# Input projections in pairs by Strassen's scheme ahead of a state-space scan

## The chip, the cores and the metric

The kernel runs on one core of one Trainium2 chip. The metric is device time in microseconds (us) of one execution; the kernel before took 2148.05 us as the median of three runs (2147.49 to 2153.19).

## What is computed

One inference step of a hybrid decoder layer, for a prompt of 1024 tokens and 8 single-token samples, 1032 rows in all, in float32:

```python
u = rmsnorm(x, norm_w)
proj = u @ w_in                      # 1024 -> 14368 columns
cb, cc, ch, cz, sz, sxbc, sdt, mq, mz, gr = jnp.split(proj, idx, axis=-1)
conv_out, new_buf_a = causal_conv(cc * ch, buf_a, conv_a_w)
y_a = (jax.nn.silu(cz) * cb * conv_out) @ w_a_out
xbc, new_buf_s = causal_conv(sxbc, buf_s, conv_s_w, conv_s_b)
...
y, h_new = ssd_scan(xs, dt, a, bm, cm, h0)
y_s = gated_rmsnorm(y + d_skip * xs, sz, ssm_norm_w) @ w_s_out
o = mem_attention(mq, mk, mv)
y_m = (jax.nn.silu(mz) * o) @ w_m_out
merged = g[:, :, 0] * y_a + g[:, :, 1] * y_s + g[:, :, 2] * y_m
return x + merged @ w_o, ...
```

In tiles of 128 columns the projection has 113 of them: 24 of xBC, 1 of dt, 16 of the scan's gate z, 8 each of cc, ch, cz and cb, 8 of q, 8 of the attention's gate and 24 of merge gates. The scan is chunked: 8 chunks of 128 tokens, 4 groups of 8 heads in each, every group adding to a state that the next chunk's group reads.

## The kernel before, in words

The program is written out engine by engine, with semaphores between them. TensorE (PE) multiplies, VectorE (DVE) does elementwise work, ScalarE (ACT) reads results out of PSUM and issues stores, GpSimd (POOL) splits weights, SyncE (SP) issues loads, all strictly in the order written.

**A projection tile** (`dense`, L195): float32 accuracy comes from a split of each operand in a high and a low part, and three products (high-high, low-high, high-low) for each of 8 blocks of the inner dimension. The 1032 rows are three pieces of 344, so a tile is 72 matmuls of 344 columns into three PSUM banks (`acc`). Its weights are loaded by SP (`load_w`, L171), split by POOL with one `tensor_scalar` and one `tensor_tensor` of 128x1024 (`split_w`, L176, L181, L183), and the pieces are read out by ACT (`read_out`, L207) or DVE.

**Order of the stages.** First the rows of x are normed, transposed and split (`turn_rows`, `high_rows`, `low_rows`); the first tile's pieces are multiplied in between. Then come the 24 xBC tiles, each followed on DVE by a four-tap convolution (L975 to L990: a `tensor_scalar` and three `scalar_tensor_tensor` of 128x1024, the same on 8 columns for the samples, and a copy of the tail), and by SiLU and a store on ACT. Then dt, two z tiles, 8 more z tiles mixed with 16 tiles of memory keys and values (product with 256 columns, tile `mhi`), transposes of keys and values, and 6 late z tiles (`late_z`). While these late tiles run, SP stores what the scan reads back (`s_cs`, `s_kt`, `s_bc`, outputs) and loads the first group.

**The scan** (PE from L1441, ACT from L795, DVE from L1112, SP from L520). For each group PE waits for `group_in` (the group's loads) and for `h_added` (the state of the group before; it frees bank `pm0`), transposes x (L1450) and b (L1452), forms the scores (L1453), runs one dense tile, transposes z (L1457), waits for DVE's masked decay matrix `mm_` (`m_ready`), does the three scan products (L1462 to L1465, `summed`), then one or two more dense tiles (`SEG`: 2, 2, 2 and 3 tiles in the groups of a chunk, 9 in all), and transposes the group's normed output (L1470). DVE for a group: decay arguments, eight `seg` rows, copies of b and scores, scaled x, `mm_` (L1119 to L1137); after `summed` the output and the state (L1143 to L1153, the state's addition is L1148), the norm's factor (L1157 to L1164), and a step of the samples' own state (`sample_step`, L1065 to L1068, in groups 0 and 2; `sample_output`, L1073 and L1075, after it). DVE also does the short convolution's arithmetic on four of the nine tiles (`dve_tile`).

SP's order in a group: x and z of the group, the decay rows broadcast to all partitions (`s_cs`), the weights of the group's tiles, and in groups 0 and 2 the sample state (`in_state_ssm`), in group 0 also the broadcast b and c of the samples (`s_bc`, 1 MB). The `s_bc` load waits until the chunk before has finished with `sd_step`, and all later loads stand behind it on SP.

**After the scan** four passes of output projections with attention beside them, and the last product with `w_o`.

Of the kernel before, what the change touches and what calls it, by code (L numbers as in the profile page):

```python
# [45 lines left out]
ZT, XT = INNER // P, XBC // P  # L46

# [17 lines left out]
def build(nc, I, O):  # L65
# [18 lines left out]
    with ExitStack() as ctx:  # L84
# [8 lines left out]
        pm = [ctx.enter_context(nc.psum_tensor(f"pm{i}", [P, 512], F32)) for i in range(5)]  # L93
        uhi = sb("uhi", [P, KT, T], F32R)
        ulo = sb("ulo", [P, KT, T], F32R)

# [12 lines left out]
        ident = sb("ident", [P, P])  # L109
        tri = sb("tri", [P, P])  # L110
        ones = sb("ones", [P, P])
        epsc = sb("epsc", [P, 1])
        par = sb("par", [P, NPAR])
        hist_s = sb("hist_s", [P, XT, NB, KS - 1])
        hist_a = sb("hist_a", [P, KT, NB, KA - 1])
        tail_s = sb("tail_s", [P, XT, TAIL_S])
        tail_a = sb("tail_a", [P, KT, TAIL_A])
        cs_tok = sb("cs_tok", [P, NCH * HEADS])
        dt_tok = sb("dt_tok", [P, NCH * HEADS])
        dskip = sb("dskip", [P, HEADS])  # L120
# [106 lines left out]
        xbc_tile = lambda i, r: (i, r, i * 3 + r)  # L227
        Q1 = XT // 3
        dt_tile, z_first = (Q1, 0, XT), [(Q1, 1, XT + 1), (Q1, 2, XT + 2)]

        mixed_tile = lambda i, j: (i * 2 + Q1 + 1 + j // 3, j % 3, None if j % 3 else i * 2 + XT + 3 + j // 3)
        late_z = lambda i, r: (i + Q1 + 9, r, i * 3 + XT + 11 + r)
        QM, FM = Q1 + 11, XT + 1 + ZT
        main_tile = lambda c, m: (c * 3 + QM + m // 3, m % 3, c * 9 + FM + m)

        xbc_src = lambda j: w_in[:, :, bass.ds(j * P + O_XBC, P)]
        z_src = lambda j: w_in[:, :, bass.ds(j * P + O_SZ, P)]
        kv_src = lambda j: w_kv[:, :, bass.ds(j * P, P)]
        MAIN = (O_CC, O_CH, O_CZ, O_CB, O_MQ, O_MZ, O_G, O_G + D, O_G + 2 * D)
        rows = lambda d, j: d[bass.ds(j * P, P), :]  # L240


        rows_in = [sem(f"rows_in{b}") for b in range(2)]
        par_in, hist_in, small_in = sem("par_in"), sem("hist_in"), sem("small_in")
        square_done, root_done, rs_done = sem("square_done"), sem("root_done"), sem("rs_done")
        normed = [sem(f"normed{b}") for b in range(2)]
        turned, u_high, u_split = sem("turned"), sem("u_high"), sem("u_split")
        par_turned, par_copied, norm_in = sem("par_turned"), sem("par_copied"), sem("norm_in")
        PROMPT_ROWS = SEQ // P + 1
        xr = [view(D), view(D)]  # L250
        xn = [view(D), view(D)]
        nwb, mwb = view(D), view(D)
        junk = view(D)
        par_rows = view(2, P)
        hrow_s, hrow_a = view(XBC), view(D)
        ssq, root, rs = view(16), view(16), view(16)
        NROW = SEQ // P + 1 + NM // P
        def row_tile(a):

            if a < SEQ // P:  # L260
                return P, I["x_prompt"][0, a * P:(a + 1) * P, :], a * P
            if a == SEQ // P:
                return NB, I["x_sample"][:, 0, :], SEQ
            a -= SEQ // P + 1
            return P, I["mem_prompt"][0, a * P:(a + 1) * P, :], a * P
        def turned_rows(a, h):

            n, _, c0 = row_tile(a)
            hi, lo = (uhi, ulo) if a < PROMPT_ROWS else (mhi, mlo)
            src = pm[2 * (a % 2) + h][:, :].rearrange("p (k c) -> p k c", c=P)[:, :, 0:n]  # L270
            return src, hi[:, 4 * h:4 * h + 4, c0:c0 + n], lo[:, 4 * h:4 * h + 4, c0:c0 + n]

        xp = view(T + KS - 1, at=M0 + 15900)
        cv = view(T)
        dtb, alog = view(1), view(1)
        conv = [sem(f"conv{k}") for k in range(KS)]
        silu_done, tails_kept, pads_ready = sem("silu_done"), sem("tails_kept"), sem("pads_ready")

# [1323 lines left out]
```

## Time and profile before

| | |
|---|---|
| median of three runs | 2148.05 us (2147.49 to 2153.19) |
| span of the profiled execution | 2154.4 us (a time of its own beside the span is not given) |
| PE busy | 2087.3 us (97%), 12986 matmuls |
| DVE busy | 1091.5 us (51%) |
| ACT busy | 563.9 us (26%) |
| POOL busy | 638.0 us (30%) |
| DMA | 299.90 MB, mean 139 GB/s |
| chain that ended last | PE 72%, DVE 11%, issue 8%, DMA 5%, ACT 3% |

Busy time of PE is the time in which some matmul is under way. Matmuls overlap, so what one costs in a row of them is the distance from one start to the next and not its duration. In a table by stretches each cell is busy us and, in brackets, the number of instructions, for PE, weight loads (PEld), DVE, ACT and POOL, then the granted TensorE clock as a share of full speed, the busy share of the DMA engines and GB/s. In a timeline the columns are start, duration, engine, line, operation, output<-input, count, and in square brackets the idle time before it and what ended that.

### The profile page before, as it was taken

The numbers are of one execution on the slowest core, as the hardware profiler recorded it, in microseconds if no ns is written. First come the engines' busy times: TensorE is split into PE (matmuls) and PEld (weight loads), VectorE is DVE, ScalarE is ACT, GpSimd is POOL, SyncE is SP. The second block draws the span as 40 slices with busy tenths as digits, with TensorE's granted clock in tenths as the row PEclk, the third lists the DMA queues.
The fourth block names the chain that finished last, engine by engine and source line by source line (L and its number), as shares of the span: only waits on it lengthen the run. The fifth ranks groups of instructions, "written<-read, shape, count | busy, mean of one in ns | idle before, by whom it ended". The sixth has DMA issues, their size and how long they took to land.

```text
span 2154.4 us, 34992 instructions
## 1 busy us (share of the span) xinstructions
PE 2087.3 (97%) x12986; PEld 1997.5 (93%) x12986; DVE 1091.5 (51%) x1894; ACT 563.9 (26%) x998; POOL 638.0 (30%) x349
## 2 busy tenths in 40 slices
PE   7999999999999999999999999999999998899998
PEld 6999999999999999999999999999989888899986
DVE  5565657201174655636465664636732455665333
ACT  4222223111224332333333333333321200201021
POOL 2232324753222232212313222321212222233800
PEclk9999999999999999999999999999999999999999
DMA  5222322446355373655446274645584776743321
GB/s 166 88 88 88 117 88 86 130 122 208 93 140 155 86 201 82 175 123 128 143 109 189 71 194 109 151 125 135 154 248 152 219 217 180 247 168 136 89 98 70
DMA packets 369543, 299.90 MB, mean 139 GB/s; under 512 B 21697, under 2 KB 337457, under 8 KB 368395
## 3 DMA queue, kind: packets, MB, share of 16 engines
q1 hardware_dynamic: 299452, 201.20, 34.4%
q10 hardware_dynamic: 70010, 97.80, 13.3%
q8 instruction: 28, 0.46, 0.1%
q14 instruction: 53, 0.43, 0.1%
HBM read 222.60 MB, written 76.59 MB: 139 GB/s over the span
## 4 chain that ended last, share of the span: by engine, by line
PE 72%; DVE 11%; issue 8%; DMA 5%; ACT 3%; ACTq 1%; DVEq 1%; POOLq 0%; POOL 0%; SPq 0%
PE acc L190 56%; PE pm L1563 5%; DMA arena<-s_qd 4%; PE pm L1464 3%; PE pm L190 2%; PE pm L1462 1%; PE pm L1465 1%; DVE arena L1263 1%; DVE arena L1150 1%; DVE arena L1144 1%; DVE arena L984 1%; PE pm L1493 1%; DVE ulo L1186 1%; DVE arena L1124 1%; ACT arena L813 1%
## 5 line engine op out<-in xcount | busy, mean ns | idle before, releaser
L190 PE MATMUL acc<-uhi,whi 128*128 128x344 f32 x3480 | 1140.5, 328 | 27.9 <-DVE ulo L1186 13.4
L190 PE MATMUL acc<-uhi,wlo 128*128 128x344 f32 x3480 | 1117.6, 321 | 0.0
L190 PE MATMUL acc<-ulo,whi 128*128 128x344 f32 x3480 | 1117.0, 321 | 0.0
L190 PEld LDWEIGHTS acc<-uhi,whi 128*128 128x128 f32 x3480 | 659.5, 190 | 42.1 <-issue 24.3
L190 PEld LDWEIGHTS acc<-uhi,wlo 128*128 128x128 f32 x3480 | 659.4, 189 | 7.9 <-issue 7.7
L190 PEld LDWEIGHTS acc<-ulo,whi 128*128 128x128 f32 x3480 | 659.2, 189 | 0.0
L181 POOL TENSOR_SCALAR whi<-raw 128x1024 fp32r<-128x1024 f32 x161 | 192.7, 1197 | 1387.1 <-PE acc L190 473.4
L183 POOL TENSOR_TENSOR wlo<-raw,whi 128x1024 fp32r<-128x1024 f32 x161 | 413.6, 2569 | 13.4
L212 ACT ACTIVATE stage<-acc 128x344 f32<-128x344 f32 x168 | 72.4, 457 | 274.7 <-PE acc L190 274.4
L1143 DVE TENSOR_TENSOR arena<-pm,arena 128x512 f32<-128x512 f32 x32 | 22.1, 691 | 167.8 <-PE pm L1465 167.8
L988 DVE SCALAR_TENSOR_TENSOR arena<-arena,par 128x1024 f32<-128x1024 f32 x72 | 92.5, 1285 | 10.4 <-DVE arena L984 0.3
L813 ACT ACTIVATE arena<-arena 128x512 f32<-128x512 f32 x32 | 20.2, 632 | 260.9 <-DVE arena L1153 260.9
L983 DVE TENSOR_SCALAR arena<-arena,par 128x1024 f32<-128x1024 f32 x24 | 29.1, 1212 | 100.8 <-ACT arena L212 100.2
L1229 DVE TENSOR_TENSOR stage<-stage,acc 128x344 f32<-128x344 f32 x72 | 35.2, 509 | 82.4 <-PE acc L190 82.4
L1464 PEld LDWEIGHTS pm<-arena 128*128 128x128 f32 x512 | 62.1, 192 | 15.4 <-issue 15.4
L840 ACT ACTIVATE uhi<-arena 128x2752 fp32r<-128x2752 f32 x9 | 22.4, 2505 | 187.1 <-DVE arena L1232 91.5
L212 ACT ACTIVATE arena<-acc 128x344 f32<-128x344 f32 x120 | 49.3, 457 | 61.7 <-PE acc L190 50.9
L1124 DVE TENSOR_SCALAR arena<-arena,cs_tok 128x128 f32<-128x128 f32 x256 | 56.0, 288 | 14.5 <-issue 14.5
L823 ACT ACTIVATE arena<-pm,par 128x128 f32<-128x128 f32 x128 | 36.6, 369 | 93.1 <-DVE stage L1111 50.0
L1464 PE MATMUL pm<-arena 128*128 128x64 f32 x512 | 60.6, 271 | 0.0
L737 ACT ACTIVATE stage<-arena 128x1032 f32<-128x1032 f32 x24 | 25.6, 1068 | 133.0 <-DVE arena L989 132.9
L212 ACT ACT_TABLE_LOAD x43 | 55.2, 1283 | 10.3 <-issue 9.7
(238 smaller groups left out, 2104.3 us busy)
## 6 DMA issues: line engine op xcount, KB each, us to landing
raw<-in_w_in SPq DMA_DIRECT2D x113, 512.0 KB, 11.4
stage<-s_g SPq DMA_DIRECT2D x32, 516.0 KB, 5.6
arena<-s_cs SPq DMA_DIRECT2D x32, 512.0 KB, 10.7
s_xbc<-stage ACTq DMA_DIRECT2D x24, 516.0 KB, 2.6
s_g<-stage ACTq DMA_DIRECT2D x24, 516.0 KB, 2.8
s_z<-stage ACTq DMA_DIRECT2D x16, 516.0 KB, 2.7
arena<-in_x_prompt SPq DMA_DIRECT2D x16, 512.0 KB, 4.0
raw<-in_w_mem_kv SPq DMA_DIRECT2D x16, 512.0 KB, 3.9
```

What stands on the lines that cost most here:

```text
L181: pool.tensor_scalar(whi[r][:], raw[r][:], 1.0, 0.0, ALU.mult, ALU.add).then_inc(w_high[r], 1)
L183: pool.tensor_tensor(wlo[r][:], raw[r][:], whi[r][:].bitcast(F32), ALU.subtract).then_inc(w_split[r], 1)
L190: mm = pe.matmul(out, w[r][:, k, :], a[:, k, c0:c0 + n], start=k == 0 and s == 0, stop=k == KT - 1 and s == 2)
L212: act.activation(out[:, p * PC:(p + 1) * PC], acc[:, p, 0:PC], func, scale=scale).then_inc(evac[p], 1)
L813: act.activation(gyn, gy, ACT.Square, accum_out=ss2).then_inc(sq2_done, 1)
L823: act.activation(yT[:, k, :], pm[2][:, k * P:(k + 1) * P], ACT.Copy, scale=par[:, C_SN + 4 * g + k:C_SN + 4 * g + k + 1]).then_inc(y_out, 1)
L983: dve.tensor_scalar(cv[:, 0:SEQ], xp[:, 0:SEQ], col(C_SW, j), col(C_SB, j), ALU.mult, ALU.add).then_inc(conv[0], 1)
L988: dve.scalar_tensor_tensor(cv[:, 0:SEQ], xp[:, k:k + SEQ], w, cv[:, 0:SEQ], ALU.mult, ALU.add).then_inc(conv[k], 1)
L1124: dve.tensor_scalar(seg[:, h, :], csb[b][:, h, :], cs_tok[:, bass.ds(c * HEADS + g * HG + h, 1)], 0.0, ALU.subtract, ALU.min).then_inc(seg ...
L1229: dve.tensor_tensor(stage[r][:, cols] if b else at, stage[r][:, cols], acc[:, p, 0:PC], ALU.mult).then_inc(evac[p], 1)
L1464: pe.matmul(pm[4][:, h * HD:(h + 1) * HD], mm_[:, h, :], xdt[:, h * HD:(h + 1) * HD], start=True, stop=True)
L1563: mm = pe.matmul(pm[2 * q + h][0:n, :], x[:, k, bass.ds(a * P, n)], w[:, half], start=k == 0 and s == 0, stop=k == KT - 1 and s == 2)
```

## The change

The 113 tiles are divided anew. 35 pairs (12 of xBC, 16 of cc/ch and cz/cb, 3 of late z, 4 of q) are computed before everything else, by Strassen's scheme: rows are halved (516), the inner dimension is halved (4 blocks) and the two tiles are the halves of the columns, so 7 half products stand for 8. Each half product is two quarters of 258 columns, 12 matmuls each: 168 matmuls of 258 columns a pair in place of 144 of 344. For it:

- Four sums of quarters of u are formed and split too (`sum_rows`, `high_sums`, `low_sums`), in 5 steps of two 104-row tiles. The first product waits until all are ready.
- For each pair POOL makes seven subtractions for low parts and four sums of weights, 11 `tensor_tensor` of 128x512; ACT makes the seven high parts.
- ACT copies three partial products out of PSUM (`keep`) and the last one (`last_out`), DVE makes three additions of two quarters each (`add`), PSUM plus SBUF.
- Convolution, gates and SiLU of xBC and of the short convolution follow the pairs, out of the scan.

In the scan each group has one dense tile (attention gate or merge gate). The transposes of a group's normed output move behind the next group's dense tile. `sample_output` moves from group 2 to group 3 for the chunk's second sample block, and the six late z tiles between key transposes and scan are gone. Cut to its core:

```diff
-        SEG = ((0, 1), (2, 3), (4, 5), (6, 7, 8))
+        HC, QC, KH, NJ = T // 2, T // 4, KT // 2, 7
+        XPOSE = ((2, 3, 0, 1), (4, 5, 6, 7))
+        SUMS = (((4, 5), (6, 7), (0, 1)), ((6, 7), (0, 1), (4, 5)))
+        MAIN = (O_MZ, O_G, O_G + D, O_G + 2 * D)
...
 SP
+            def next_pair(v, b, srcs):
+                sp.wait_ge(b_split, v * 2 * NB_STEPS + (b - 1) * NB_STEPS)
+                settle(sp)
+                load_pair(v, b, srcs)
...
-            with sp.Fori(0, 2) as i:
-                for r in range(3):
-                    load_w(sp, late_z(i, r), z_src(i * 3 + 10 + r))
...
-                    for m in SEG[g]:
-                        load_w(sp, main_tile(c, m), w_in[:, :, bass.ds(c * P + MAIN[m], P)])
+                    load_w(sp, main_tile(c, g), cols_of(MAIN[g], c))
...
 POOL
+            def low_slot(v, b, j):
+                pool.wait_ge(b_high, v * 2 * NJ + (b * NJ + j + 1))
+                settle(pool)
+                pool.tensor_tensor(slot(blo, j), source_of(b, j), slot(bhi, j).bitcast(F32), ALU.subtract).then_inc(b_split, 1)
...
+            def split_pair(v, b):
+                low_slot(v, b, 0)
+                first_sums(v, b)
+                for j in (1, 2, 3):
+                    low_slot(v, b, j)
+                third_sum(v, b)
+                for j in (4, 5):
+                    low_slot(v, b, j)
+                fourth_sum(v, b)
+                low_slot(v, b, 6)
+            def low_sums(s):
+                n = step_cols(s)[1]
+                c0 = s * SR
+                for x, i in enumerate((IS_S1, IS_S3, IS_S2, IS_S4)):
+                    pool.wait_ge(u_high, s * 9 + 5 + x + 1)
+                    pool.tensor_tensor(slo[:, i * KH:(i + 1) * KH, c0:c0 + n], t_of[i][:, :, 0:n],
+                                       shi[:, i * KH:(i + 1) * KH, c0:c0 + n].bitcast(F32), ALU.subtract).then_inc(s_low, 1)
...
 ACT
+            def high_u(s):
...
+                if s:
+                    act.wait_ge(s_low, 4 * s)
...
+            def act_pair(v, b, last, after, nxt=True):
+                for j in range(NJ):
+                    if j in KEEP:
+                        keep(v, b, j)
+                    if j == NJ - 1:
+                        last()
+                    if nxt:
+                        act.wait_ge(multiplied, v * 4 * NJ + (b * 2 * NJ + 2 * j + 2))
+                        high_slot(v + b, 1 - b, j)
+                    for step in after.get(j, ()):
+                        step()
...
 DVE
+            ADDS = {1: (1, p1, 1, 0), 4: (0, p5, 5, 2), 5: (2, u2, 3, 4)}
+            def add_pair(v, b, first, second):
+                add(v, b, 1, first[:, 0:HC])
+                add(v, b, 4, second[:, HC:T])
+                add(v, b, 5, second[:, 0:HC])
...
+            def xbc_pair(v, b, opening=False):
+                if not opening:
+                    dve.wait_ge(conv, v * 36 + b * 18)
+                add_pair(v, b, xp[0][:, KS - 1:], xp[1][:, KS - 1:])
+                all_added(v, b)
+                conv_xbc(v, b, 1, opening)
+                conv_xbc(v, b, 0, opening)
...
                     if g % 2 == 0:
                         sample_step(c, g)
                     if g == 1:
                         sample_output(c, 0)
-                    for m in SEG[g][1:]:
-                        dve_tile(c, m)
-                    if g == 2:
+                    if g == 3:
                         sample_output(c, 2)
...
 PE
+            def pair_step(v, b, j):
+                x, y, z = SUMS[b]
+                to = (x, y, x, z, x, z, x)[j]
+                first = j in (0, 1, 3)
...
+                pe.wait_ge(b_split, v * 2 * NB_STEPS + (b * NB_STEPS + LOW_AT[j]))
+                for q in range(2):
+                    pe.wait_ge(prior[0], prior[1] + q)
+                    for k in range(KH):
+                        hi, lo = moving(j, k, q)
+                        for i, (w, m) in enumerate(((bhi, hi), (blo, hi), (bhi, lo))):
+                            mm = pe.matmul(bank[to[q]][:, 0:QC], w[:, j * KH + k, :], m, start=first and k == 0 and i == 0,
+                                           stop=k == KH - 1 and i == 2, skip_group_check=True)
+                    mm.then_inc(multiplied, 1)
...
+            pe.wait_ge(u_low, 8 * STEPS)
+            pe.wait_ge(s_low, 4 * STEPS)
+            pair_step(0, 0, 0)
...
+            def ssd_group(c, g, first=False):
+                n, b, u = c * 4 + g, g % 2, c * 2 + g // 2
+                bg, cg = xg[b][:, 4, :], xg[b][:, 5, :]
+                pe.wait_ge(group_in[b], (u + 1) * 64)
+                pe.wait_ge(h_added, n + 1)
+                for k in range(4):
+                    tr = pe.transpose(pm[0][:, k * P:(k + 1) * P], xg[b][:, k, :], ident[:])
+                tr.then_inc(x_turned, 1)
...
+                dense(pe, main_tile(c, g))
+                if not first:
+                    pe.wait_ge(bt_ready, n + 1)
+                    pe.wait_ge(sc_ready, n + 1)
+                    turn_y(c if g else c - 1, (g - 1) % GROUPS)
+                pe.wait_ge(gy_ready, n + OPEN)
...
+                pe.wait_ge(m_ready, n + 1 + OPEN)
+                pe.wait_ge(xdd_ready, n + 1)
+                pe.wait_ge(bt_ready, n + 1)
+                pe.matmul(pm[3][:], cg, hT[:, g, :], start=True, stop=True)
+                for h in range(HG):
+                    pe.matmul(pm[4][:, h * HD:(h + 1) * HD], mm_[:, h, :], xdt[:, h * HD:(h + 1) * HD], start=True, stop=True)
+                pe.matmul(pm[0][:], bt, xdd, start=True, stop=True).then_inc(summed[b], 1)
```

## Rows read from the trace of the kernel before

**Rows 1.** Busy time of each engine by stretches that follow the stages.
```profile
0.00:321.90 321.90, 295.38 (x1833) 290.73 (x1834) 188.90 (x248) 96.30 (x157) 96.29 (x63) 0.98 0.33 105
...
493.70:566.80 73.10, 73.10 (x484) 72.70 (x483) 10.03 (x27) 12.24 (x22) 22.30 (x13) 1.00 0.62 189
566.80:1557.80 991.00, 985.85 (x6302) 948.96 (x6301) 565.45 (x1084) 341.29 (x612) 270.03 (x144) 1.00 0.50 135
1557.80:1570.70 12.90, 8.37 (x41) 6.87 (x39) 10.78 (x18) 5.18 (x11) 0.00 (x0) 0.74 0.82 225
```

**Rows 2.** Timeline of PE where matmuls of 344 and of 256 columns follow each other.
```profile
367.25 0.32 PE L190 MATMUL acc<-uhi,whi 128*128 128x344 f32 x1
...
369.13 0.29 PE L190 MATMUL pm<-mhi,whi 128*128 128x256 f32 x1
...
373.93 0.28 PE L190 MATMUL pm<-mlo,whi 128*128 128x256 f32 x1
```

**Rows 3.** Timeline of PE in the scan, from one group's transposes to its second ones.
```profile
718.79 0.60 PE L1450 MATMUL pm<-ident,arena 128*128 128x128 f32 x4
...
719.48 0.40 PE L190 MATMUL acc<-uhi,whi 128*128 128x344 f32 x1
...
730.89 0.60 PE L1457 MATMUL pm<-ident,arena 128*128 128x128 f32 x4
```

**Rows 4.** Timeline of DVE in the scan, parts of three groups.
```profile
707.22 0.69 DVE L1143 TENSOR_TENSOR arena<-pm,arena 128x512 f32<-128x512 f32 x1 [7.88 <-PE pm L1465]
...
709.03 0.68 DVE L1148 TENSOR_TENSOR arena<-arena,pm 128x512 f32<-128x512 f32 x1
...
716.94 1.23 DVE L1068 TENSOR_TENSOR arena<-arena 128x1024 f32<-128x1024 f32 x1
...
777.02 3.32 DVE L1068 TENSOR_TENSOR arena<-arena 128x1024 f32<-128x1024 f32 x1
...
782.88 0.15 DVE L1119 TENSOR_TENSOR arena<-arena,cs_tok 128x8 f32<-128x8 f32 x1
...
786.46 1.22 DVE L1137 TENSOR_TENSOR arena<-arena 128x1024 f32<-128x1024 f32 x1
...
791.78 0.69 DVE L1143 TENSOR_TENSOR arena<-pm,arena 128x512 f32<-128x512 f32 x1 [3.50 <-PE pm L1465]
```

**Rows 5.** Timeline of POOL at the time of the long DVE row above.
```profile
776.00 3.26 POOL L183 TENSOR_TENSOR wlo<-raw,whi 128x1024 fp32r<-128x1024 f32 x1
```

**Rows 6.** Groups by shape: DVE from 46 to 322 us, POOL over the span.
```profile
L988 DVE SCALAR_TENSOR_TENSOR arena<-arena,par 128x1024 f32<-128x1024 f32 x69 | 88.7, 1285 | 10.0 <-DVE arena L984 0.3
...
L983 DVE TENSOR_SCALAR arena<-arena,par 128x1024 f32<-128x1024 f32 x23 | 28.1, 1224 | 97.5 <-ACT arena L212 96.9 <-DVE hist_a L967 0.6
...
L183 POOL TENSOR_TENSOR wlo<-raw,whi 128x1024 fp32r<-128x1024 f32 x161 | 413.6, 2569 | 13.4
```

**Rows 7.** Timelines of SP and DVE while the scan's first group is loaded.
```profile
519.68 0.45 SPq L529 DMA_DIRECT2D arena<-s_cs  x1
...
531.24 0.17 DVE L1119 TENSOR_TENSOR arena<-arena,cs_tok 128x8 f32<-128x8 f32 x1 [9.64 <-DMA arena<-s_cs]
```

**Rows 8.** A weight load in the page's list of DMAs; SP's timeline in the scan.
```profile
raw<-in_w_in SPq DMA_DIRECT2D x113, 512.0 KB, 11.4
...
793.44 0.37 SPq L543 DMA_DIRECT2D arena<-in_state_ssm  x1
...
796.67 5.54 SPq L174 DMA_DIRECT2D raw<-in_w_in  x2
```

**Rows 9.** A PE wait in its timeline, and the stretch right after it.
```profile
1743.35 0.99 PE L1502 MATMUL pm<-ident,arena 128*128 128x128 f32 x4 [2.35 <-DVE arena L1250]
...
1743.50:1747.00 3.50, 3.50 (x16) 3.50 (x16) 2.22 (x4) 1.20 (x2) 0.00 (x0) 0.51 0.77 151
```

**Rows 10.** Groups by shape in the opening: ACT's squares, DVE's low parts of u.
```profile
L713 ACT ACTIVATE arena<-arena 128x1024 f32<-128x1024 f32 x10 | 10.5, 1054 | 4.3 <-DMA arena<-in_x_prompt 3.5 <-ACT stage L737 0.7
...
L955 DVE TENSOR_TENSOR ulo<-pm,uhi 128x512 fp32r<-128x512 f32 x16 | 10.2, 681 | 4.1 <-ACT uhi L720 4.1
```

More of the change, by code:

```diff
@@ L266, in turned_rows @@
[L266 to L277, printed above, removed]
+        NROW = TILES + NM // P
@@ L514, in _ @@
             sp.wait_ge(bc_saved, 16 * 16)
[L515 removed]
+            for r, n in enumerate((8, 1, 1)):
                 sp.wait_ge(stored[r], 16 * n + OPEN)
@@ new lines, in _ @@
+            low_slot(0, 0, 0)
+            pool.wait_ge(par_turned, 1)
+            first_sums(0, 0)
+            low_slot(0, 0, 1)
+            low_sums(2)
+            low_slot(0, 0, 2)
+            low_slot(0, 0, 3)
+            third_sum(0, 0)
+            low_sums(3)
+            low_slot(0, 0, 4)
+            low_slot(0, 0, 5)
+            fourth_sum(0, 0)
+            low_sums(4)
+            low_slot(0, 0, 6)
+            split_pair(0, 1)
+            with pool.Fori(1, PAIRS // 2) as v:
+                for b in range(2):
+                    split_pair(v, b)
@@ new lines, in silu_half, with gate_last, save_a @@
+            def silu_half(c):
+                for q in range(2):
+                    act.wait_ge(added, (c + V1) * 12 + (6 + ADDED + 1 + q))
+                act.activation(cv[1][:, 0:HC], cv[1][:, 0:HC], ACT.Silu).then_inc(silu_done, 1)
+            def gate_last(c):
+                act.wait_ge(c_saved[1], c * 16 + 16 * XP)
+                last_out(c + V1, 1, cv[1][:, HC:], ACT.Silu)
+            def save_a(c):
+                save(cv[1], rows(s_a, c), gate_step, c * 10 + 10, c_saved[1])
@@ L771, in _ @@
             act.activation(dd[0:HEADS, 0, :], da[0:HEADS, SEQ:], ACT.Exp).then_inc(dd_ready, 1)
-            with act.Fori(0, 2) as i:
-                for r in range(3):
-                    to_dram(act, late_z(i, r), i + (Q1 + 8 if r == 0 else Q1 + 1), rows(s_z, i * 3 + 10 + r), ACT.Silu)
             act.wait_ge(kv_saved, 48)
@@ L828, in high_part @@
+            for g in range(GROUPS):
+                act_group(0, g, g == 0)
+            with act.Fori(1, NCH) as c:
+                for g in range(GROUPS):
+                    act_group(c, g)
+            scale_y(NCH - 1, GROUPS - 1)
             def high_part(b, p):
@@ new lines, in _ @@
+            conv_a(0, True)
+            gate_a(0)
+            with dve.Fori(1, KT) as c:
+                conv_a(c)
+                gate_a(c)
+            V2 = (XP + CP) // 2
+            dve.wait_ge(gate_step, 10 * KT)
+            for k in range(FP):
+                bufs = (xp, cv)[k % 2]
+                if k % 2:
+                    for n in range(2):
+                        dve.wait_ge(c_saved[n], 16 * (k // 2 + XP + (KT if n else 0)))
+                elif k:
+                    dve.wait_ge(x_saved, 32 * (k // 2))
+                add_pair(V2 + k // 2, k % 2, bufs[0], bufs[1])
```

840 lines of the change are left out of this document (499 added, 341 removed).

## The prediction, written before the change was run

> **What bounds the kernel now.** I read the page first: PE is busy nearly all the span and the chain of waits lies mostly on it, so the question is where PE would lose its cover. The table by stretches shows it by stage [rows 1]: the opening with the 24 xBC tiles (321.9 us), a stretch of dt, z and mixed tiles (171.8, from the borders), 73.1 us of key transposes and late z tiles with PE busy throughout, 991.0 us of scan with PE busy in 985.85, a tail of 12.9, and 583.7 us of attention and output passes, which the change leaves alone. In the scan DVE has 565 us of work and is hidden by two or three projection tiles per group. So anything that shortens PE's stream pays in full, until a chain through DVE, or a load, is no longer covered. The timelines of PE, DVE, POOL and SP give the lengths of those chains.
>
> **What a pair saves.** PE starts 12 matmuls of 344 columns in 1.88 us, 0.157 each, and 41 of 256 columns in 4.80 us, 0.117 each [rows 2]; 258 columns take 0.118. A tile before is 72 x 0.157 = 11.3 us, which the scan's timeline confirms as 11.4 from the first matmul to the next transposes [rows 3]; two tiles are 22.7. A Strassen pair is 168 x 0.118 = 19.8, so it saves 2.9 us, not the eighth of a product alone, since the columns cost a little more each.
>
> The Trainium skill ("TensorE: Matmul & The Clock Gate", section "Back-to-back issue gap") gives a gap of N/2.4 + 2.5 ns at full clock. By it 258 columns are 110 ns and 344 are 146: a pair 18.5 against 21.0, a saving of 2.5 us, some 14 us less over 35 pairs. The trace's 0.157 is 7% above its figure, and the measurement decides.
>
> **The sum**, against the profiled span of 2154.4, which is 6.3 us (0.3%) above the median:
>
> 1. **Opening.** Before, what isn't a tile in the first stretch is 321.9 - 24 x 11.37 = 49 us [rows 1, 3]. Now the first product waits for four extra sums of u in 5 steps. One step in series: two squares 2.1 (1054 ns each), five copies of 416 columns 2.8 and four sums 2.2 and the last copy 0.55 (0.55 each, from 681 ns for 512), then four POOL subtractions of 416 columns, 4.2 (2569 ns for 1024) [rows 6, 10]. That is 11.8; the next step's copies wait for POOL's sums, so 5 steps and one to fill: 71 us. Bounds 49 (all overlapped) and 90 (loads of rows between the steps).
> 2. **xBC pairs.** PE needs 19.8. POOL's 11 operations of 128x512 are 11 x 1.28 = 14.1. The convolution of two tiles on DVE is 2 x (1.22 + 3 x 1.285) [rows 6] and three small ones of 0.15 (a 128x8 operation [rows 4]), 10.6. These exclude each other [rows 5]: POOL's subtraction ends at 779.26, DVE's operation that began at 777.02 [rows 4] took 3.32 in place of 1.23 and ended 1.1 after POOL's. If they run one at a time a pair takes 24.7 and PE waits for low parts. 12 x 24.7 = 296; bounds 19.8 (238) and 28 (336, POOL waits at each handover too). Steps 1 and 2: 367 for 321.9, **+45**.
> 3. **The other 23 pairs.** Per two pairs POOL has 28 and DVE's excluding work about 8, less than PE's 39.6, so PE binds and ACT's high parts and copies are beside it: 23 x 19.8, **+455**; with a us of waiting in each, +23.
> 4. **dt to mixed tiles.** Their small loads now stand on SP behind the last stores of the pairs: **+3**.
> 5. **Before the scan.** The six late z tiles covered SP's stores and reloads. From the last key tile (493.7) SP needs until 531.2, when the first group's decay rows are there [rows 7]: 37.5 bare for 73.1 [rows 1], **-35.6** (30 to 42 saved).
> 6. **The scan.** With one tile a group, a ring closes. PE's x transposes now wait for the state of the group before, because the state's product leaves in bank `pm0`. After the products, DVE's state addition (L1148) ends 2.5 us after the output's first operation (707.22 to 709.71) [rows 4]; then transposes 0.7 and the tile 11.4 [rows 3]; the transposes of y and z 0.9 (estimate, two sets like 718.79's); and 4.1 from the finished mask to the output's first operation (787.68 to 791.78) [rows 4]: 19.6. DVE's own ring is as long: from that operation to the end of the sample step 10.95 (707.22 to 718.17), decay to mask 4.8 (782.88 to 787.68), and 4.1: 19.85 [rows 4]. So 19.7. Each group PE now stands still about 2.5 us; after a wait of 2.35 its granted clock was 0.51 (the 1.2 GHz level) for 3.5 us [rows 9], so I add 1.5: 21.2, and 32 groups are 676. Before, a group was 31.0.
>    The loads come on top. On SP the `s_bc` load waits for `sample_output`, now in group 3, about 10.95 after the state's product (like the sample step above); everything for group 1 is queued behind: 3.2 us from the sample state's issue to the weights' issue, 11.4 until they land [rows 8], about 3.5 for the split (2.57 and the high part, estimate). 29 to 33 us, where PE wants that tile after 21.2 + 3.2 = 24.4. The sample state of group 2's half does the same a little less late to group 3. I take 10 us a chunk, 74 in all (7 chunks and 4); bounds 0 (landed in time) and 15. Scan 750 for 991, **-241**; bounds 627 (19.6 a group, no late load) and 790.
> 7. **Tail.** The last group's DVE work and the first activations' split lose the two tiles that lay over them: 21 for 12.9, **+8** (to +17).
> 8. The rest: 0; its order on each engine stands as before.
>
> +45 + 455 + 3 - 35.6 - 241 + 8 = +234: 2389 in a profile, 2383 as a median. In short: 40 tiles leave the scan, worth 455 of PE time; only 241 come back, because the scan was filled to 99% by them and is now bound by its own ring.
>
> What is queued behind the new waits: behind `h_added` on PE the transposes and the tile itself, and so the whole next group; behind `s_bc` on SP all loads; behind ACT's wait for `b_high`'s sources (POOL's sums) its copies `keep`, and through them DVE's additions and PE's banks.
>
> **Rivals.**
> - **Loads land in time and the clock stays up.** Group 19.7 without 1.5 and without 74: 676 + 74 becomes 627, the whole 2261. For it: loads have a two-group lead by buffers. Against it: SP's order in front of the weights. Chance 0.2.
> - **POOL and DVE don't exclude each other over the xBC pairs**, because the convolution falls between POOL's operations: 19.8 a pair, 58 less, 2325. Against it: 24.7 of work into 19.8 needs an overlap that the trace doesn't show [rows 5]. Chance 0.15. Both of these together: about 2200, 0.07.
> - **The other side: PE hides everything.** If the state's addition were done before PE gets to the x transposes, a group would be PE's own work, 11.4 + 0.7 + 0.9 + 4 = 17.0, so scan 544; with the opening at 60 and pairs at 19.8: 60 + 238 - 321.9 + 455 + 3 - 35.6 - 447 + 8 = -41, 2114 in a profile and 2107 as a median. The change wins only if a group takes under about 18.3 with these; against it stands a state addition that ends 2.5 us after the products, with nothing for PE to do in between. Chance 0.08.
> - **The Strassen pairs don't save**: at 344 columns' rate per column 258 would be 0.118 too, so this can hardly be; a stall in each half product (PSUM copies late) would add 1 us a pair, 35 in all, which lies in the upper end.
>
> The Trainium skill ("SBUF — State Buffer", section "SBUF: two separate sides") calls the port pair of VectorE and GpSimd an exclusive lock for a whole instruction. The trace agrees, 3.32 for 1.23 [rows 4, 5]; by the rule without exception step 2 is 24.7 a pair and speaks against the change, without it 19.8.
>
> **The numbers.** The forecast has 0.5. The range, 2220 to 2480, holds it with its bounds (opening to 90, pairs at 28 or a us of waits in each of 23, chunk waits at 15: up to about 2480), and the two single rivals; it leaves out the other side, most of both together and the worst sums. Faster by over 0.3% 0.08, within 0.3% (about what a measurement of this kernel can tell from no change) 0.03, slower 0.89.
>
> **What would show it.** Right: starts of 258 columns 0.118 apart; a first product at about 71 us; a period of about 25 in xBC pairs with DVE's convolution rows near 2.4 us where before they have 1.3 [rows 6]; 37 us of an idle PE before the scan; groups of about 21 us with PE idle before the x transposes, released by DVE's state addition, a granted clock below 1.0 in the scan, and long PE waits on the weights' split in two groups of a chunk. Wrong: a scan with PE above 95% busy and groups near 17 us, or xBC pairs at 19.8, or weights that wait for PE and not the other way.

## The result and the profile after

The kernel after takes 2457.55 us as the median of four runs (2447.2 to 2459.8) against 2149.16 before: a ratio of 1.1425, 95% interval 1.1399 to 1.145. The profiled execution has a span of 2445.3 us, 290.9 above that of before. The forecast was 2383 with a range of 2220 to 2480: the direction and most of the size are there, and some 56 us of the profiled loss were not in the sum.

The table by stretches of the kernel after, cut where the stages begin and end (opening; 12 xBC pairs; 23 other pairs; dt to mixed tiles; before the scan; scan; tail; rest), with columns as in [rows 1]:

```profile
0.00:65.04 65.04, 16.59 (x82) 13.61 (x83) 39.51 (x61) 39.84 (x84) 36.41 (x41) 1.00 0.43 113
65.04:387.40 322.36, 268.76 (x2029) 264.32 (x2030) 242.10 (x275) 107.22 (x200) 197.13 (x130) 0.91 0.23 74
387.40:866.25 478.85, 469.76 (x3887) 469.17 (x3885) 177.39 (x238) 177.39 (x365) 337.10 (x247) 0.99 0.23 73
866.25:1045.16 178.91, 173.87 (x1192) 173.46 (x1193) 48.83 (x33) 32.00 (x63) 96.82 (x52) 0.99 0.39 122
1045.16:1077.00 31.84, 5.20 (x51) 4.63 (x50) 8.16 (x16) 1.88 (x3) 0.00 (x0) 0.62 0.57 162
1077.00:1829.50 752.50, 600.67 (x3416) 555.05 (x3417) 436.99 (x963) 308.61 (x534) 124.16 (x64) 0.86 0.53 138
1829.50:1863.40 33.90, 12.09 (x46) 9.51 (x45) 26.89 (x28) 6.78 (x14) 9.21 (x4) 0.65 0.74 231
1863.40:2445.30 581.90, 553.16 (x3142) 507.62 (x3140) 265.49 (x486) 76.81 (x133) 153.48 (x77) 0.97 0.51 163
```

Against before [rows 1] and against the forecast:

| stage | before | after | difference | forecast |
|---|---|---|---|---|
| opening and xBC | 321.9 | 387.4 | +65.5 | +45 |
| other pairs | 0 | 478.9 | +478.9 | +455 |
| dt to mixed | 171.8 | 178.9 | +7.1 | +3 |
| before the scan | 73.1 | 31.8 | -41.3 | -35.6 |
| scan | 991.0 | 752.5 | -238.5 | -241 |
| tail | 12.9 | 33.9 | +21.0 | +8 |
| rest | 583.7 | 581.9 | -1.8 | 0 |

The scan gives back half of what leaves it. In it PE's granted clock fell from 1.00 to 0.86, and PE is idle for 152 of 752 us. What PE waited for in the whole span (us in total, times, longest):

```profile
PE pm L1760 <- DMA arena<-s_cs: 68.9, 13, 26.6
PE acc L210 <- POOL wlo L203: 59.5, 16, 7.1
PE pm L1680 <- DVE room L1214: 58.3, 12, 8.4
PE pm L1760 <- DVE arena L1426: 50.1, 19, 2.7
...
PE pm L1799 <- DMA arena<-s_q: 10.6, 1, 10.6
...
PE pm L1749 <- ACT arena L1043: 7.9, 1, 7.9
```

L1760 is a group's x transposes, L210 a tile's first matmul, L1680 a half product, L1214 DVE's additions for the pairs, L1426 DVE's state addition. The longest of the s_cs waits, 26.6, is the one before the scan; the other twelve and the sixteen on the split weights lie in the scan.

**An xBC pair** takes 27.5 us in the steady state (ten periods from PE's wait that ends at 111.95 to the one that ends at 386.81) and not 24.7, and PE does not wait where I had put it. PE's timeline, the start of a pair's seventh and last half product and two later starts:

```profile
304.71 0.58 PE L1680 MATMUL pm<-uhi,bhi 128*128 128x258 f32 x1 [4.60 <-DVE room L1214]
305.09 0.42 PE L1680 MATMUL pm<-uhi,blo 128*128 128x258 f32 x1
305.30 0.42 PE L1680 MATMUL pm<-ulo,bhi 128*128 128x258 f32 x1
...
310.02 0.28 PE L1680 MATMUL pm<-uhi,blo 128*128 128x258 f32 x1
...
312.30 0.28 PE L1680 MATMUL pm<-ulo,bhi 128*128 128x258 f32 x1
```

It waits for the additions, and after the wait it starts one matmul each 0.21 us, the 1.2 GHz level, until some 4 us later the starts are 0.12 apart (19 intervals from 310.02 to 312.30). DVE's timeline, with two rows of POOL's, shows why the additions are late: they stand behind both convolutions of the pair before.

```profile
303.56 1.42 DVE L1214 TENSOR_TENSOR room<-pm,psb 128x258 f32<-128x258 f32 x4 [0.24 <-DVE room L1242]
304.90 0.75 DVE L1214 TENSOR_TENSOR room<-acc,psb 128x258 f32<-128x258 f32 x2
310.39 0.17 DVE L1232 COPY tail_s<-room 128x11 f32 x1 [4.74 <-ACT room L875]
...
313.90 1.26 DVE L1242 SCALAR_TENSOR_TENSOR room<-hist_s,par,room 128x8 f32<-128x8 f32 x1
315.31 2.28 DVE L1241 SCALAR_TENSOR_TENSOR room<-room,par 128x1024 f32<-128x1024 f32 x1
...
324.59 0.22 DVE L1242 SCALAR_TENSOR_TENSOR room<-hist_s,par,room 128x8 f32<-128x8 f32 x1
...
331.04 0.76 DVE L1214 TENSOR_TENSOR room<-acc,psb 128x258 f32<-128x258 f32 x2 [0.21 <-DVE room L1242]
```

```profile
313.77 1.37 POOL L728 TENSOR_TENSOR blo<-wraw,bhi 128x512 fp32r<-128x512 f32 x1 [1.25 <-ACT bhi L832]
315.22 1.29 POOL L733 TENSOR_TENSOR wraw<-wraw 128x512 f32<-128x512 f32 x1
```

From 310.4 to 330.8 the two convolutions take 20.4 us. A large tap costs 2.28 where it meets POOL and 1.28 where not [rows 6], and a tap of 128x8 columns 1.26 in place of 0.22. The one at 313.90 began just behind a subtraction of POOL's and ended with it: a small operation pays for nearly a whole operation of POOL.

**A scan group** follows the forecast's ring. PE's timeline, the x transposes of two groups and the tile between them:

```profile
1285.85 1.11 PE L1760 MATMUL pm<-ident,arena 128*128 128x128 f32 x4 [4.17 <-DMA arena<-s_cs]
...
1291.11 0.65 PE L210 MATMUL acc<-uhi,whi 128*128 128x344 f32 x1 [3.51 <-POOL wlo L203]
...
1311.65 0.63 PE L1760 MATMUL pm<-ident,arena 128*128 128x128 f32 x4 [2.67 <-DVE arena L1426]
```

SP's timeline ahead of the first of these, the sample state, then the group's loads and its weights:

```profile
1271.57 0.37 SPq L599 DMA_DIRECT2D arena<-in_state_ssm  x1
1272.19 0.38 SPq L583 DMA_DIRECT2D arena<-s_xbc  x1
...
1276.26 1.48 SPq L194 DMA_DIRECT2D raw<-in_w_in  x1
```

Where the state binds, PE waits 2.67; every second group waits for what SP issued right behind the sample state.

### The profile page after: what moved, and what is told of

It reads as the page before. It is cut to its first block, busy times and chain, and to the rows that moved or that the text cites. A ratio compares the mean times of both kernels' runs of the same rounds, so it can differ in the third digit from the quotient of the medians.

```text
span 2445.3 us, 39533 instructions
## 1 busy us (share of the span) xinstructions
PE 2100.1 (86%) x13834; PEld 1997.4 (82%) x13834; DVE 1245.4 (51%) x2096; ACT 750.5 (31%) x1394; POOL 954.3 (39%) x613
## 4 chain that ended last, share of the span: by engine, by line
PE 54%; DMA 12%; DVE 6%; SPq 3%; issue 3%; POOL 2%; ACT 1%; ACTq 1%; DVEq 0%; POOLq 0%
PE acc L210 25%; PE pm L1680 14%; DMA raw<-in_w_in 7%; PE pm L1879 4%; PE acc L1680 4%; DMA arena<-s_qd 4%; PE pm L210 2%; POOL wlo L203 2%; PE pm L1780 1%; DVE arena L1539 1%; DVE arena L1389 1%; DVE arena L1391 1%; SPq L586 1%; POOL whi L201 1%; PE pm L1809 1%
## 5 line engine op out<-in xcount | busy, mean ns | idle before, releaser
L210 PE MATMUL acc<-uhi,whi 128*128 128x344 f32 x1800 | 611.1, 340 | 73.3 <-POOL wlo L203 59.5
L210 PE MATMUL acc<-uhi,wlo 128*128 128x344 f32 x1800 | 600.8, 334 | 0.0
L210 PE MATMUL acc<-ulo,whi 128*128 128x344 f32 x1800 | 599.6, 333 | 0.0
L210 PEld LDWEIGHTS acc<-uhi,whi 128*128 128x128 f32 x1800 | 363.1, 202 | 80.0 <-issue 71.9
L728 POOL TENSOR_TENSOR blo<-wraw,bhi 128x512 fp32r<-128x512 f32 x210 | 296.9, 1414 | 236.4 <-ACT bhi L832 236.4
L210 PEld LDWEIGHTS acc<-uhi,wlo 128*128 128x128 f32 x1800 | 361.4, 201 | 0.2
L210 PEld LDWEIGHTS acc<-ulo,whi 128*128 128x128 f32 x1800 | 360.7, 200 | 0.0
L1680 PE MATMUL pm<-uhi,bhi 128*128 128x258 f32 x704 | 212.6, 302 | 69.7 <-DVE room L1214 58.3
L1680 PE MATMUL pm<-shi,bhi 128*128 128x258 f32 x832 | 235.6, 283 | 2.1 <-ACT psb L870 2.1
L1680 PE MATMUL pm<-slo,bhi 128*128 128x258 f32 x832 | 235.3, 283 | 0.0
L1680 PE MATMUL pm<-shi,blo 128*128 128x258 f32 x832 | 234.8, 282 | 0.0
L1680 PE MATMUL pm<-uhi,blo 128*128 128x258 f32 x704 | 210.1, 298 | 0.0
L1680 PE MATMUL pm<-ulo,bhi 128*128 128x258 f32 x704 | 209.4, 297 | 0.0
L1680 PEld LDWEIGHTS pm<-uhi,bhi 128*128 128x128 f32 x704 | 145.4, 207 | 72.5 <-DVE room L1214 56.3
L1680 PEld LDWEIGHTS pm<-shi,bhi 128*128 128x128 f32 x832 | 157.5, 189 | 3.4 <-ACT psb L870 2.9
L1214 DVE TENSOR_TENSOR room<-pm,psb 128x258 f32<-128x258 f32 x140 | 56.3, 424 | 203.4 <-PE pm L1680 198.3
L1680 PEld LDWEIGHTS pm<-slo,bhi 128*128 128x128 f32 x832 | 157.5, 189 | 0.0
L1680 PEld LDWEIGHTS pm<-shi,blo 128*128 128x128 f32 x832 | 157.4, 189 | 0.0
L1680 PEld LDWEIGHTS pm<-uhi,blo 128*128 128x128 f32 x704 | 145.5, 207 | 0.0
## 6 DMA issues: line engine op xcount, KB each, us to landing
arena<-s_cs SPq DMA_DIRECT2D x32, 512.0 KB, 11.4
```

Source lines behind the costliest of these rows:

```text
L210: mm = pe.matmul(out, w[r][:, k, :], a[:, k, c0:c0 + n], start=k == 0 and s == 0, stop=k == KT - 1 and s == 2)
L728: pool.tensor_tensor(slot(blo, j), source_of(b, j), slot(bhi, j).bitcast(F32), ALU.subtract).then_inc(b_split, 1)
L1214: dve.tensor_tensor(piece(dst, q), bank[SUMS[b][s_of][q]][:, 0:QC], piece(other, q), ALU.add).then_inc(added, 1)
L1680: mm = pe.matmul(bank[to[q]][:, 0:QC], w[:, j * KH + k, :], m, start=first and k == 0 and i == 0, stop=k == KH - 1 and i == 2, skip_group_ ...
```

## The experiments

Each version was run once, except e9 and e13 with four runs each. The scan of the same code took 753 to 773 us in the profiles of runs that left it alone, so these runs are read by the stage that they change, and whole times only from 20 us on. The pairs are steadier: the xBC stage took 324 to 326 us, from its first product to the first of the next stage, in the seven profiles that leave it alone.

**e1: POOL's subtractions left out in ten of the xBC pairs** (there the second line stands for the first).

```diff
-                pool.tensor_tensor(slot(blo, j), source_of(b, j), slot(bhi, j).bitcast(F32), ALU.subtract).then_inc(b_split, 1)
+                pool.memset(slot(blo, j)[:, 0:1, 0:1].bitcast(F32), 0.0).then_inc(b_split, 1)
```

> Leaves out POOL's seven subtractions for low parts in 10 of the 12 xBC pairs (a one-element memset stands for each; the four sums of weights stay). Theory A (in an xBC pair the two convolutions on DVE, held up by POOL's operations, delay the next pair's additions and PE waits for those): without POOL beside it a pair's convolutions take some 11 us and not 20, PE has no wait for DVE's additions left, a pair takes PE's 20.2 in place of 26.8, the span falls by 10 x 6.6 = 66 us. Rival B (the sums of u and the copies out of PSUM on ACT set the pace, or DVE's convolutions are long by themselves): pairs stay above 24, at most 25 us gained.

Measured: 2384.95 us. The stretch of the xBC pairs, first product to last addition:

```profile
64.60:314.80 250.20, 245.86 (x2028) 245.49 (x2029) 184.00 (x275) 106.42 (x200) 97.32 (x130) 0.99 0.29 96
```

250 us for 322, and 20.1 a pair in the ten that were changed: what the other pairs take. PE's waits for the additions fall from 58.3 to 12.7 and the clock comes back to 0.99. Theory A holds; B is out. Its size for the convolutions was off: two of them still take 14.5 us (212.4 to 226.9) and not 11, since taps still meet POOL's sums.

**e2: three of four small taps left out, POOL whole.**

```diff
-                    dve.scalar_tensor_tensor(y[:, SEQ:], now, w, y[:, SEQ:], ALU.mult, ALU.add).then_inc(conv, 1)
+                    dve.sem_inc(conv, 1)
```

> Leaves out three of the four small taps (128x8, the samples' columns) of every xBC convolution on DVE; POOL's work stays whole. Theory A: these small operations cost 1.25 us where POOL holds them up and 0.15 where not; six per pair gone are worth up to 7 us, PE's wait for additions (4.85 us a pair) and the half-rate stretch after it go, a pair takes 20 to 22 us, the span falls by 55 to 75. Rival B (POOL's own chain, its waits for ACT's high parts, sets the pace): POOL's work is the same, a pair stays at 25 to 27.

Measured: the stage took 287.2 us, 24.2 a pair, 35 us less; the time was 2424.18. That lies between the 20 to 22 of theory A and the 25 to 27 of rival B, and PE still waits 2.9 a pair for the additions. So leaving the small taps out gives back about half of the 72 us of e1. The size was off: without them POOL meets the large taps instead, and I had not reckoned with that. Three of them in a row, 1.28 each when free:

```profile
214.37 5.74 DVE L1241 SCALAR_TENSOR_TENSOR room<-room,par 128x1024 f32<-128x1024 f32 x3 [0.15 <-DVE room L1238]
```

**e6: sums in PSUM.** Two banks are free during the pairs. Each tap of 1024 columns becomes two of 512 with one operand in PSUM:

```diff
-                    dve.scalar_tensor_tensor(y[:, 0:SEQ], x[:, k:k + SEQ], w, y[:, 0:SEQ], ALU.mult, ALU.add).then_inc(conv, 1)
+                    for h in range(2):
+                        src = x[:, k + h * 512:k + h * 512 + 512]
+                        dve.scalar_tensor_tensor(ysum[h], src, w, ysum[h], ALU.mult, ALU.add).then_inc(conv, 1)
...
```

> The 1024 columns of the xBC convolutions are summed in two free PSUM banks instead of SBUF, so that each tap reads only one operand from SBUF; POOL's work and the small taps stay, ACT's SiLU reads PSUM, and the second tile of a pair waits for the SiLU of the first. Theory A (POOL holds up DVE's taps because both operands of a tap lie in SBUF): the taps take 2 x 0.68 each with POOL beside them, a pair falls from 26.8 to 20 to 22 us, the xBC stage from 323 to 245 to 265. Rival B (the handover to ACT between the two tiles, or the small taps, take the place of the held-up ones): a pair stays at 24 to 27.

Measured: 2413.76 us, the stage 282.9, 23.2 to 24.7 a pair: between the two theories. DVE's timeline, and a row of POOL's:

```profile
211.91 1.01 DVE L1257 SCALAR_TENSOR_TENSOR room<-hist_s,par,room 128x8 f32<-128x8 f32 x1
213.06 0.76 DVE L1253 SCALAR_TENSOR_TENSOR acc<-room,par,acc 128x512 f32<-128x512 f32 x1
213.72 0.75 DVE L1253 SCALAR_TENSOR_TENSOR pm<-room,par,pm 128x512 f32<-128x512 f32 x1
...
218.67 0.81 DVE L1251 TENSOR_SCALAR acc<-room,par 128x512 f32<-128x512 f32 x1 [1.54 <-ACT room L900]
```

```profile
212.97 1.29 POOL L735 TENSOR_TENSOR wraw<-wraw 128x512 f32<-128x512 f32 x1
```

The large taps now pass POOL at 0.75 each (0.76 is the longest in the run); small ones still pay up to 1.2, and the handover to ACT costs 1.5. With 23.7 a pair is still dearer than two tiles of before at 22.7, so for xBC the scheme does not pay even then.

**e3: sample-state loads behind the next group's loads.**

```diff
-                    if g % 2 == 0:
-                        if g == 0:
+                    if g % 2:
+                        if g == 1:
                             sp.wait_ge(sd_step, c * 10 + OPEN)
```

> Puts SP's loads of the sample state and of the samples' b and c (with their waits) behind the next group's loads. Theory C (in groups 1 and 3 of each chunk the weights come late because SP stands at these waits): PE's wait for the split weights, 59.5 us in 16 places, is gone, every second group falls from 25 to 21 us, the scan from 752 to about 680, the span by 60 to 75. Rival D (the weights are late because of the transfer itself, or because their buffer comes free late): less than 15 us.

Measured: 2371.09 us. The stretch of the scan:

```profile
1077.40:1755.30 677.90, 577.96 (x3420) 533.12 (x3420) 466.82 (x963) 307.12 (x534) 130.39 (x64) 0.93 0.60 154
```

PE's waits, in the columns of the list above:

```profile
PE pm L1760 <- DVE arena L1426: 82.2, 31, 2.7
...
PE pm L1760 <- DMA arena<-s_cs: 26.5, 1, 26.5
```

752.5 became 677.9: theory C, 75 us (up to 95 against the slowest scan of unchanged code). In the scan the waits for weights and for decay rows are gone, but for one of 3.4 in the first group, and every group now waits 2.7 for the state: 677.9 / 32 = 21.2 us a group. The mask (L1417) became longer by it, 2.22 on average for 1.22 in the kernel after: POOL's split of the weights now falls on 19 of the 32 masks, and before on none.

**e5: e3 and a third of the tile ahead of the state wait.**

```diff
+                dense(pe, main_tile(c, g), pieces=(0, 1))
                 pe.wait_ge(group_in[b], (u + 1) * 64)
                 pe.wait_ge(h_added, n + 1)
...
-                dense(pe, main_tile(c, g))
+                dense(pe, main_tile(c, g), pieces=(1, NP))
```

> The same as the run with SP's loads reordered, and PE does the first of the tile's three pieces ahead of its wait for the state of the group before. Theory E (PE's ring binds: state wait, transposes, tile, products in series): the piece, 3.8 us, covers the wait of 2.7, the clock stays up, a group falls from 21 to 17.5 to 18.5, the scan to 560 to 600, the span another 80 to 110 below the reordered one. Rival F (DVE's ring is as long, as I forecast with 19.85): the wait moves to the finished mask, groups stay at 19.5 to 21, the span falls by less than 45 more.

Measured: 2383.92 us; the scan 680.7 from its first transposes, no shorter than in e3. The stretch before it is 12 us longer than in e3, since the piece there waits 32.2 for its split weights, where the transposes waited 26.5. PE's wait for the state is gone, and another stands in its place in the list of PE's waits:

```profile
PE pm L1780 <- DVE arena L1418: 72.4, 30, 4.3
```

L1418 is the mask. The timelines of DVE and POOL show one:

```profile
1412.60 3.36 DVE L1418 TENSOR_TENSOR arena<-arena 128x1024 f32<-128x1024 f32 x1
```

```profile
1412.22 2.66 POOL L203 TENSOR_TENSOR wlo<-raw,whi 128x1024 fp32r<-128x1024 f32 x1
```

Rival F: the wait moved to the mask and the group stayed at 21. Groups alternate between about 18 and 24 to 27 us, nearly all the long ones following a sample step; the mask itself took 3.36 here for 1.22 [rows 4], while POOL split the next tile's weights. 21 of the 32 masks took 2.06 or more, and they are those that POOL's split met; the ten of 3.36 are all in long groups. So the ring that binds here has these meetings with POOL in it; the forecast's 19.85 has none.

**e11: e5 with the samples' state on 4 of its 128 columns.**

```diff
-                dve.tensor_tensor(sd, sd, sd2, ALU.add).then_inc(sd_step, 1)
+                dve.tensor_tensor(sd[:, :, few], sd[:, :, few], sd2[:, :, few], ALU.add).then_inc(sd_step, 1)
...
```

> On top of the run with reordered loads and one piece of the tile ahead of the state wait, whose groups stayed at 21 with PE waiting for the mask: DVE does the samples' state (step in groups 0 and 2, output in 1 and 3) on 4 of its 128 columns, so 5 operations of 1.2 us become some 0.2; nothing else changes. Theory F (DVE's ring binds there, the samples' state being in it): every group loses 2.1 to 3.1 us of the ring, the scan falls from 681 to 590 to 610. Rival M (what binds is the latency from the x transposes through ACT and DVE to the mask, which the samples' state does not lengthen, or POOL's split holding up the mask): the scan falls by less than 35.

Measured: 2243.65 us. The scan:

```profile
1086.80:1632.90 546.10, 529.55 (x3398) 489.65 (x3396) 328.46 (x953) 303.57 (x534) 107.04 (x62) 1.00 0.72 188
```

546 us, 17.1 a group, the clock at 1.00 (0.90 in e5): PE's own work, which I had put at 17.0. The fall of 135 us is far beyond the 35 of rival M and beyond theory F's 71 to 91, so DVE's ring did bind in e5. But not the samples' state alone went. DVE's busy time over the scan fell by 140 us, from 468.9 to 328.5: 80 are the samples' five operations, and 60 are the mask and the operation behind it, of which only one still meets POOL's split. The mask in e5 and in e11:

```profile
L1418 DVE TENSOR_TENSOR arena<-arena 128x1024 f32<-128x1024 f32 x32 | 69.6, 2176 | 0.0
```

```profile
L1420 DVE TENSOR_TENSOR arena<-arena 128x1024 f32<-128x1024 f32 x32 | 39.0, 1219 | 0.0
```

That is 4.4 us less DVE work a group and 4.2 us less a group. How much of it the samples' state would give with the meetings left in, or the meetings alone (rival M's second half), e11 does not tell.

**e12: e5 with the samples' state in full, between mask and products.**

```diff
+                    if g % 2 == 0:
+                        sample_step(c, g)
...
                     dve.wait_ge(summed[b], u + 1 + OPEN)
...
-                    if g % 2 == 0:
-                        sample_step(c, g)
```

> As the run with reordered loads and one piece ahead of the state wait, with the samples' state in full, but DVE does it between the finished mask and the scan products, where it stands waiting for PE, instead of ahead of the next group's decay rows. Theory F (what binds is where these operations lie in DVE's ring, not that they are done): DVE's wait of 3.4 us for the products takes them in, a group falls from 21.3 to 17.1 to 18.5, the scan to 550 to 595, the time to 2250 to 2290. Rival N (their mere length on DVE, or the memory's load for them coming late, binds): the scan stays above 640.

Measured: 2331.31 us, the scan 639.5: 41 less than e5, and not the 90 or more that I expected; rival N had its bound at 640. DVE now waits for the state's load:

```profile
1415.69 1.23 DVE L1382 TENSOR_TENSOR arena<-arena 128x1024 f32<-128x1024 f32 x1 [6.54 <-DMA arena<-in_state_ssm]
```

Over the scan these waits come to 63.7 us. SP issues this load behind the group's loads and `s_bc`, at 1404.46, 8 us after the first of them, and it lands 11 us later. So rival N's second half, the late load, took the place of the wait for the products. A second buffer for the state was not tried.

**e7: four late z tiles back before the scan,** two pairs fewer.

```diff
-XP, CP, FP = XT // 2, 2 * KT, 7
+XP, CP, FP = XT // 2, 2 * KT, 5
...
+            for i in range(2):
+                for r in range(2):
+                    dense(pe, late_z(i, r))
```

> Undoes one part: four of the late z tiles go back between the key transposes and the scan as ordinary tiles, two pairs less are done up front. Theory G (the 31 us before the scan are SP's bare chain, and any tile put there is free up to that length): pairs fall by 2 x 20.2 = 40 us, the stretch before the scan grows from 31 to some 46, the span falls by 22 to 28. Rival H (the tiles' loads and splits delay SP's chain by as much): less than 10 us.

Measured: 2422.47 us. The other pairs, from their first product to the last, fell by 40.3 (474.4 to 434.1). The stretch from the first key transposes to the scan grew by 18.4, from 30.7 to 49.1, with PE busy all through: 22 less, theory G.

```profile
1005.20:1054.30 49.10, 49.10 (x323) 48.80 (x323) 10.01 (x26) 7.30 (x14) 10.67 (x7) 1.00 0.75 218
```

**e8: e3, e6 and e7 together.**

> Three changes together: sums of the convolutions in PSUM, sample-state loads behind the next group's loads, four late z tiles back before the scan. If the three losses are separate, as theories A, C and G have it, the gains add: 65 + 76 + 24 = 165, the time is 2290 to 2300, still 140 above the kernel before, of which some 70 are scan groups bound by PE's and DVE's rings, 16 the opening and 20 the tail. If they share a cause (the clock, or SP's queue), the sum is 40 us or more smaller.

Measured: 2310.4 us with a span of 2308.7, 136.6 below that of the kernel after, where 165 were expected with e6 at 65. With the 40 that e6's stage gave alone the sum is 75 + 22 + 40 = 137. That the two agree to within a us is luck, given how the scan varies; but each stage is near its time in the single run (xBC, first product to first product, 287.3 and 286.4; scan 684.1 and 677.9; before the scan 49 in both): the losses are separate.

**e9: e8 with the eight q tiles back in the scan.**

```diff
                 pe.matmul(pm[0][:], bt, xdd, start=True, stop=True).then_inc(summed[b], 1)
+                if g == 1:
+                    dense(pe, q_tile(c))
...
```

> On top of the three changes together: the eight q tiles go back into the scan as ordinary tiles, a second one in group 1 of every chunk behind the scan products; four pairs less are done up front. Theory I (a group with one tile leaves PE about 4 us idle in its ring, which a second tile fills): the pairs fall by 4 x 20.2 = 81 us, a group with two tiles takes 28.4 in place of 21.2, 8 of them add 58, the time falls by 20 to 30, to about 2285. Rival J (the ring's time is bound elsewhere, or the tile's load comes late, so the tile costs its 11.4 or more): the scan grows by 91 or more, the time does not fall.

Measured: 2288.37 us (2283.35 to 2296.75), ratio to before 1.0657 (1.0621 to 1.0692). The other pairs fell by 80.9 and the scan grew by 59.7, 7.5 a tile in place of 11.4: theory I. A tile in a scan bound by its ring is cheaper than its half of a Strassen pair (10.1).

**e10: one load of the tail earlier on SP.**

```diff
             first_acts(0)
+            sp.dma_start(qx, s_q[:, SEQ:].rearrange("(t p) b -> p t b", p=P)).then_inc(S["qx_in"], 16)
             sp.wait_ge(sd_step, 80 + OPEN)
...
-            sp.dma_start(qx, s_q[:, SEQ:].rearrange("(t p) b -> p t b", p=P)).then_inc(S["qx_in"], 16)
             sp.wait_ge(y_turned, 32 + OPEN)
```

> In the changed kernel itself, one load (the samples' q) is issued on SP ahead of the waits for the samples' state, instead of behind them and two weight loads. Theory K (the 32.6 us between scan and first output tile hold 10.6 of PE waiting for this load): the tail falls by 6 to 11. Rival L (the first activations' split on DVE, which ends at about the same time, is the real end of the chain): PE's wait moves to that, less than 4 us.

Measured: the tail, here from the last scan product to the first output tile, 31.7 for 32.6; the whole time, 2463.65, did not fall. Neither theory: PE's wait went to the next load in SP's order, which had cost it 2.0.

```profile
PE pm L1809 <- DMA arena<-s_kt: 11.0, 1, 11.0
```

**e13: e12, e6 and e7 together.**

> The same with the convolutions' sums in PSUM and four late z tiles back before the scan. If all the losses found are separate: 37 and 24 us less again, 2190 to 2230; against the kernel before it is still slower, by the opening (15), the tail (18) and pairs that save 2.6 us each on 21 of them while the xBC pairs cost more than two tiles. A time below 2149 would need the scan at 480, less than PE's own work of 17 us a group.

Measured: 2269.9 us (2266.9 to 2274.77), ratio 1.0564 (1.0544 to 1.0584). The scan is 645, near e12's 639.5, which is why it is above the 2190 to 2230 expected: that range reckoned with a scan of 550 to 595. From e12's measured 2331 the 37 and 24 lead to 2270. No version of the change beat the kernel before.

## Why the prediction was right, and where its sum was not

- **The saving of a pair**: 0.120 a start, 20.1 a pair outside xBC, so 2.6 saved for the 2.9 forecast: the 0.118 that I scaled from 256 columns was 0.002 too low, 168 times. The Trainium skill ("TensorE: Matmul & The Clock Gate", section "Back-to-back issue gap") makes 110 ns for 258 columns, by the formula that it gives for the gap of an isolated matmul; the trace is 9% above it, and 7% with 344. The saving by that rule, 2.5, was nearer than mine, though both of its times are too low.
- **Opening**: 65.0 for 71. No run took it apart.
- **xBC pairs**, the step that failed most: forecast 24.7 a pair, measured 27.5 and for the stage 322 against 296. The mutual exclusion was right (e1: 20.15 without POOL's subtractions), but the step put PE's wait at the low parts, as a sum of two engines' work. It lies at DVE's additions, which stand behind 20.4 us of convolution where I had 10.6. I had counted three small operations in a pair, at 0.15; there are eight, and six of them pay 1.2 or more in the pair shown. After the wait comes the stretch at the lower clock. The Trainium skill ("SBUF — State Buffer", section "SBUF: two separate sides") names the shared port pair; by its rule the loser waits for the whole instruction, and both e1 and the small taps (1.26 for 0.22) agree. The taps with an operand in PSUM (0.75 beside POOL, e6) fit it too.
- **Other pairs**: 478.9, the upper bound, but by luck and not by the us of waiting in each that the bound stood for: 22 of the 23 pairs start 20.15 us apart, with no wait. Of the 23.5 us over 455.4, 8 are the spacing (23 x 0.35) and 10.9 the first pair behind xBC, which takes 31.0 with a wait of 8.4 and a stretch at the lower clock. The rest, some 4, is the border: the table cuts at 387.4, and the first of these pairs starts at 391.3.
- **Before the scan**: right within 6 us, and e7 shows that much of the stretch is free room (four tiles, some 45 us at 11.37, added 18.4).
- **The scan**: 752.5 for 750. PE's ring is as forecast: a group without late loads took 21.2 for 21.2 (e3; 32 of them are 678, not the 676 of the sum), with a wait of 2.67 for the state where the forecast had about 2.5. Late loads came where they were forecast, in every second group by SP's order; that their 74 met 75 (e3) is luck, since the 10 us a chunk were a choice between 0 and 15 and the scan of the same code varies by 20. That DVE's ring is as long is shown only in part: with the state wait covered it binds at 21 (e5), but with POOL's split on the mask, which the 19.85 does not contain. The rival in which loads land and the clock stays up did not come; when e3 let the loads land, the clock was still 0.93. Only with DVE relieved and a piece moved (e11) did a group come to 17.1, PE's own work, as "PE hides everything" has it. The kernel of e11, which leaves most of the samples' state out, is still at 2243.65.
- **Tail**, +21 for +8 and beyond its bound of +17: I counted DVE's rest and the split, and left out SP's order. PE's wait of 10.6 is for a load of q that stands on SP behind two waits and two weight loads, and e10 only moved the wait to the next load.
- **The account**: 40 tiles left the scan, 455 us at 11.37 each, and six left the stretch before it. The 23 pairs that took these 46 over cost 479; the scan shrank by 238.5 and the stretch before it by 41. e9 turns this around for eight tiles.
- **The range**: most misses lie on one side (xBC +26, other pairs +24, tail +13 against -6 for the opening and for the stretch before the scan), so the time came out near the upper end of the range, which 2 us more in each xBC pair would have passed.

## What to carry to other kernels

A cheaper product saves only the difference per unit (2.6 us in 22.7 here); before moving work out of a stage in which it covers a chain, price that chain, ring by ring, at one unit of cover. Work that fills a ring's idle time costs less there (7.5 for 11.4) than in its cheaper form elsewhere. When two engines exclude each other, look at the smallest operations first, and when a wait is removed, ask which engine's ring is the next longest: here covering PE's wait (e3 to e5) left the group at 21 us on DVE's ring, and moving DVE's work (e12) brought out a load.

## What the runs showed of the hardware

- A tap of 128x8 on DVE took 1.26 us beside POOL's operations on SBUF and 0.22 without; with an accumulator in PSUM, a tap of 512 columns took 0.75 beside them, and 0.76 at most in the whole run (e6).
- After a wait of 4.6 us PE started its matmuls 0.21 us apart for about 4 us, then 0.12. From e5 to e11 the granted clock over the scan went from 0.90 to 1.00, with 4.4 us less DVE work and 4.2 us less time a group.
